# Openings of a fused two-block kernel: several output tiles side by side while h's rows come, x in four transfers and squared as it lands

## The reference, cut to what matters

```python
h = rmsnorm(x, norm_gain)                  # x * rsqrt(mean(x*x) + 1e-6) * gain
proj = h @ w_in                            # 1024 x 7956, split over four mixers
...                                        # four mixers -> ys
mixed = sum(sigmoid(merge[i]) * (ys[i] @ w_branch[i]))
x = rmsnorm(x + mixed @ w_out, final_gain)
for l in range(2):                         # second block, two layers
    h = rms_norm(x, norm_mix_g[l]) * (1 + scale_m) + shift_m
    proj = h @ w_in[l]                     # queries, keys, values, gates
    ...                                    # two attentions, gates, w_out
    x = x + gate_m * y
    h = rms_norm(x, norm_mlp_g[l]) * (1 + scale_f) + shift_f
    x = x + gate_f * (relu(h @ w_mlp_up[l])**2 @ w_mlp_down[l])
```

## Time and profile before

| | us |
|---|---|
| median of 3 runs | 2796.71 (2793.35 to 2798.49) |
| the profiled execution's own time | 2806.41 |
| its span, first to last instruction | 2804.7 |
| PE busy in the span | 2584.9 (92%) |
| DVE busy | 1627.1 (58%) |
| ACT busy | 1056.1 (38%) |
| mean granted TensorE clock | 0.952 of full speed |

### The profile page before, as it was taken

How to read it: one execution, slowest core, us unless ns; L and a number is a source line. 1 busy time by engine, 2 the same in 40 slices (tenths; PEclk the granted TensorE clock), 3 DMA queues, 4 the chain that set the end, 5 groups by cost and what they waited for, 6 DMA issues and landing times. The chain is left out here.

```text
span 2804.7 us, 37803 instructions
## 1 busy us (share of the span) xinstructions
PE 2584.9 (92%) x14861; PEld 2061.8 (74%) x14861; DVE 1627.1 (58%) x3102; ACT 1056.1 (38%) x2170; POOL 22.1 (1%) x68
## 2 busy tenths in 40 slices
PE   6998687899989999889989999898999899899999
PEld 4886577688767668767768888687577677688887
DVE  5645666887665686343477775563873533544444
ACT  3235422433455365442332222353653522422221
POOL 0001000000000000000000000000000000000000
PEclk8997898899989999999999999899999999899999
DMA  4220110576312201303335553121003032223220
GB/s 152 80 60 1 35 35 3 187 219 199 124 60 65 90 1 46 81 25 98 108 136 192 196 192 108 60 91 60 31 16 87 26 94 90 89 90 113 98 91 30
DMA packets 212218, 249.42 MB, mean 89 GB/s; under 512 B 13551, under 2 KB 125898, under 8 KB 212042
## 3 DMA queue, kind: packets, MB, share of 16 engines
q1 hardware_dynamic: 185504, 195.87, 21.8%
q10 hardware_dynamic: 26538, 51.14, 5.3%
HBM read 243.57 MB, written 2.10 MB: 88 GB/s over the span
## 5 line engine op out<-in xcount | busy, mean ns | idle before, releaser
L2558 ACT ACTIVATE weights_hi<-weight_ring 128x512 fp32r<-128x512 f32 (+1 forms) x240 | 143.8, 603 | 402.2 <-PE bank L2614 374.5
L2580 DVE TENSOR_TENSOR weights_lo<-weight_ring,weights_hi 128x512 fp32r<-128x512 f32 (+1 forms) x240 | 155.5, 652 | 223.4 <-ACT weights_hi L2558 223.3
L3205 ACT ACTIVATE weights_hi<-weight_ring 128x1024 fp32r<-128x1024 f32 x128 | 135.3, 1057 | 257.1 <-PE bank L3300 255.8
L2614 PE MATMUL bank<-h_hi,weights_hi 128*128 128x512 f32 x512 | 208.9, 408 | 14.8 <-DVE h_lo L2580 8.5
L3300 PE MATMUL bank<-h_hi,weights_hi 128*128 128x512 f32 x512 | 203.1, 397 | 13.2 <-DVE h_lo L422 12.3
L2614 PE MATMUL bank<-h_lo,weights_hi 128*128 128x512 f32 x512 | 204.4, 399 | 0.0
L3300 PE MATMUL bank<-h_lo,weights_hi 128*128 128x512 f32 x512 | 203.5, 397 | 0.0
L2775 PE MATMUL bank<-chunk_hi,h_hi 128*128 128x512 f32 x448 | 185.6, 414 | 18.1 <-DVE h_lo L422 15.5
L2614 PE MATMUL bank<-h_hi,weights_lo 128*128 128x512 f32 x512 | 202.0, 395 | 0.0
L3300 PE MATMUL bank<-h_hi,weights_lo 128*128 128x512 f32 x512 | 200.8, 392 | 0.0
L3300 PE MATMUL bank<-hidden_hi,weights_hi 128*128 128x512 f32 x512 | 199.4, 389 | 0.0
(11 more groups left out here) (495 smaller groups left out, 5407.5 us busy)
## 6 DMA issues: line engine op xcount, KB each, us to landing
arena<-in_ada_w ACTq DMA_DIRECT2D x48, 1024.0 KB, 5.2
weight_ring<-in_w_in SPq DMA_DIRECT2D x21, 2048.0 KB, 8.1
weight_ring<-in_w_in SPq DMA_DIRECT2D x65, 512.0 KB, 5.3
weight_ring<-in_w_mlp_up SPq DMA_DIRECT2D x16, 2048.0 KB, 9.2
weight_ring<-in_w_mlp_down SPq DMA_DIRECT2D x16, 2048.0 KB, 7.9
weight_ring<-in_w_out SPq DMA_DIRECT2D x6, 2048.0 KB, 7.9
weight_ring<-in_w_in SPq DMA_DIRECT2D x10, 1024.0 KB, 8.3
weight_ring<-in_w_branch_a SPq DMA_DIRECT2D x16, 512.0 KB, 6.4
```

Source lines behind the costliest of these rows:

```text
L2558: act.activation(hi, src, ACT.Copy).then_inc(*hi_done.one())
L2580: dve.tensor_tensor(lo, src, hi.bitcast(F32), ALU.subtract).then_inc(*lo_done.one())
L2614: ins = pe.matmul(out, ws[a_][:, n % PIECES, k - k0, :], tile["x"][b_][:, k, :], start=k + a_ + b_ == 0, stop=last[n] and k == k1 - 1 and ...
L3205: act.activation(ws[0][:, t % 2], src[t // 4][:, :, c % 4 * P:c % 4 * P + P], ACT.Copy)\
```

## The change

x comes in four transfers of 256 columns each, PE transposes as they land, and ACT squares and DVE adds each row behind its copy, in `load`. The block `rms` is gone: the product with ones, the mean and the root stand at the head of `first_projection`, and the first chunk's weights are split between h's rows. In `first_projection` PE works on the first chunk's four tiles side by side: for each row k, 12 matmuls. In `queries_keys` with a norm it works on three units side by side (9 matmuls per row), and turns lag 3 steps in place of 2. In `mlp` it works on two tiles side by side (6 per row); both weight splits are made first. In `split_products` with a norm DVE scales rows 0 to 3, makes piece 0's splits, and scales rows 4 to 7 after them.

```diff
 # load
-                pe.wait_ge(*self.x_landed.all_of_stage(16))
                 for k in range(ND):
+                    if k % (ND // PARTS) == 0:
+                        pe.wait_ge(*self.x_parts[k * PARTS // ND].at(16))
...
                     dve.tensor_copy(self.xT[:, k, :], self.bank[k][:]).then_inc(*self.evac_dve.one())
+                    if k >= 2:
+                        squares.add(dve, k - 1)
+                squares.add(dve, ND - 1)
...
+                act.preload_act_table_set(LN_AND_EXP)
+                for k in range(ND):
+                    act.wait_ge(*self.evac_dve.at(k + 1))
+                    squares.square(act, k, self.xT[:, k, :])
...
-                sp.dma_start(x_tm, a["x"][0].rearrange("(i p) d -> p i d", p=P)).then_inc(*self.x_landed.dma())
+                for j in range(PARTS):
+                    cols = slice(j * width, (j + 1) * width)
+                    sp.dma_start(x_tm[:, :, cols], a["x"][0].rearrange("(i p) d -> p i d", p=P)[:, :, cols])\
+                      .then_inc(*self.x_parts[j].dma())
-    def rms(self, name, gain, rs):
...
 # first_projection
+                norm.sums(pe)
+                opening = last.index(True) + 1
...
+                for k in range(ND):
+                    pe.wait_ge(*h_split.at(k + 1))
+                    self.w.wait_parts(pe, ("p1", name), k)
+                    for t in range(opening):
+                        lo = tiles[t][3]
+                        for a_, b_ in ((0, 0), (1, 0), (0, 1)):
+                            ins = pe.matmul(self.bank[t][:], w[b_][:, k, lo:lo + P], h[a_][:, k, :], start=k + a_ + b_ == 0,
+                                            stop=k == ND - 1 and b_ == 1)
...
+                self.w.split_hi(act)
+                norm.root(act)
                 for k in range(ND):
+                    if k % 2 == 0 and k < ND - 2:
+                        self.w.split_hi(act)
                     norm.first_part(act, h[0][:, k, :], k).then_inc(*h_first.one())
...
+                norm.mean(dve)
+                self.w.split_lo(dve)
+                norm.vector_and_second(dve, second, piece)     # piece: split_lo at k 2, 4, 6
...
 # split_products
-                if norm is not None:
-                    norm.vector(dve)
+                for k in range(ND // 2 if norm is not None else 0):
+                    norm.vector_row(dve, k)
...
+                    for k in range(ND // 2, ND if norm is not None and n == 0 else 0):
+                        norm.vector_row(dve, k)
...
 # queries_keys
+                def opening():
+                    for k in range(ND):
+                        pe.wait_ge(*h_split.at(k + 1))
+                        self.w.wait_parts(pe, key, k)
+                        for i in range(3):
...
-                steps((0, project), (2, turn), beside=lambda step: guest.tensor(pe, step))
+                if norm is None:
+                    steps((0, project), (2, turn), beside=lambda step: guest.tensor(pe, step))
+                else:
+                    opening()
+                    steps((0, lambda n, c, i: project(n, c, i) if n >= 3 else None), (3, turn))
...
 # mlp
                 split(0)
+                split(1)
                 self.norm.root(act)
...
-                    if t + 1 < N:
+                    if t and t + 1 < N:
                         split(t + 1)
...
+                split(0)
                 self.norm.mean(dve)
-                split(0)
+                split(1)
...
+                for k in range(ND):
+                    pe.wait_ge(*lo_done.at(k + 3))
+                    for t in range(2):
+                        for a_, b_ in ((0, 0), (0, 1), (1, 0)):
+                            ins = pe.matmul(self.bank[t][:], ws[a_][:, t, k, :], hs[b_][:, k, :], start=k + a_ + b_ == 0,
+                                            stop=k == ND - 1 and a_ == 1)
```

More of the change, by code:

```diff
@@ L345, in __init__ @@
         self.scaled, self.shifted = kernel.scaled, kernel.shifted
-        self.squares, self.first_mean = squares, first_mean
+        self.squares, self.first_mean, self.open = squares, first_mean, True
     def sums(self, pe):
@@ L380, in vector_row @@
     def vector_row(self, dve, k):
-        if k == 0 and self.squares is not None:
+        if k == 0 and self.open:
             dve.wait_ge(*self.kernel.root_done.at(1))
@@ L883, in __init__ @@
         self.x_landed = Signal(nc, "x_landed")
+        self.x_parts = [Signal(nc, f"x_part_landed_{j}") for j in range(4)]
         self.mm_done = Signal(nc, "mm_done")
@@ L968, in load @@
         rows = self.take(2, P)
+        PARTS = 4
+        width = D // PARTS
+        squares = Squares(self)
         with nc.Block() as block:
@@ L1022, in load @@
         self.end_stage("load")
-    def rms(self, name, gain, rs):
[L1028 to L1063, removed]
-                    self.w.split_lo(dve)
-                dve.wait_ge(*self.mm_done.at(1))
-                dve.tensor_scalar(rs, self.bank[0][:], 1.0 / D, EPS, ALU.mult, ALU.add)\
-                   .then_inc(*self.dve_ready.step("mean"))
-                for _ in range(pieces - pieces // 2):
-                    self.w.split_lo(dve)
-            @block.sync
-            def _(sp):
-                self.w.feed(sp)
-        self.top = keep
-        self.end_stage(name)
@@ L1078, in first_projection @@
+        return squares
     def first_projection(self):
@@ L1167, in _ @@
             def _(pe):
+                norm.sums(pe)
+                name = tiles[0][0]
+                opening = last.index(True) + 1
+                w = self.w.parts(("p1", name))
+                assert opening <= NB and all(tile[1] == "features" for tile in tiles[:opening])
+                for k in range(ND):
[6 more added lines that the diff above has]
+                                            stop=k == ND - 1 and b_ == 1)
+                        if k == ND - 1:
+                            ins.then_inc(*self.mm_done.one())
+                self.w.release(self.mm_done)
                 for t, (name, kind, i, lo, n) in enumerate(tiles):
+                    if t < opening:
+                        continue
                     key = ("p1", name)
@@ L2748, in queries_keys, with steps @@
         h, h_first, h_split = self.split_h, self.shifted, self.pool_ready
-        def steps(*stages, beside):
+        def steps(*stages, beside=None):
             for step in range(max(N + max(lag for lag, _ in stages), guest.LAST if guest else 0)):
@@ L2779, in project @@
                         self.w.release(pe_done)
+                def opening():
+                    key = chunks[0][0]
+                    w = self.w.parts(key)
+                    for k in range(ND):
+                        pe.wait_ge(*h_split.at(k + 1))
+                        self.w.wait_parts(pe, key, k)
+                        for i in range(3):
+                            for a_, b_ in ((0, 0), (1, 0), (0, 1)):
+                                ins = pe.matmul(self.bank[i][:, 0:width], h[a_][:, k, i * P:(i + 1) * P], w[b_][:, k, :],
+                                                start=k + a_ + b_ == 0, stop=k == ND - 1 and b_ == 1)
+                            if k == ND - 1:
+                                ins.then_inc(*pe_done.one())
                 def turn(n, c, i):
```

32 lines of the change are left out of this document (17 added, 15 removed).

## The result

| | before | after |
|---|---|---|
| median, us | 2799.43 (10 runs, 2793.35 to 2808.32) | 2791.51 (10 runs, 2789.29 to 2800.36) |
| ratio after / before | | 0.9968, 95% interval 0.9957 to 0.9979 |
| span of the profiled execution | 2804.7 | 2789.9 |
| mean granted clock | 0.952 | 0.957 |

The change is faster by 0.32% by the ratio, 9.0 us with an interval from 5.9 to 12.0, and by 7.9 us between the two medians; I had forecast 11.9 us and 2784.8. The two profiled spans differ by 14.8 us, nearly twice what the medians say, so a single pair of traces can't be read as the result. I go through the stages first and come back to this.

A forecast was written before the change was run, and what follows sets the result against it. PE, 92% busy, was taken to bound the kernel. Terms -8.9 - 4.5 - 5.1 + 2.65 + 2.1 + 1.85 = -11.9 us, off 2796.7, gave 2784.8 us; range 2777 to 2792.5.

The forecast's parts named there:

- The start: Load to h's first row: quartered x brings that row at 21.7 against 29.25, 7.5 us earlier; bounds 6 and 9.
- The fixed cost of about 2.0 us: x's transfers: if paid in series, the last quarter lands about 6 us later and the sum is about -9.5.
- The first projection's opening: First projection, four tiles side by side: done at 48.2 against 57.1, -8.9 us, 7.5 of them from the earlier start.
- The low clock: Start of an opening: 3.7 us at low clock from its first matmul, 8.7 matmuls, when PE always has work.
- Queries and keys: Queries and keys, both layers, three units side by side: -4.5 and -5.1 us net, from 6.7 and 7.2 saved.
- what is given back: Behind the queries' openings: waits of 0.4 for a scale, 1.3 for a weight piece, 0.45 for the later turn; 2.15 together.
- Rival C: All openings: the clock stays at 0.5 through them, +58 us less 11.9, giving 2843; chance 0.03.
- Merge: Merge: four rows scaled behind the guest's transfer make each later piece 2.65 us later, +2.65 us.
- Feed-forwards: Feed-forwards, both layers: two tiles side by side and the queue ahead of tile 2 cost +2.1 and +1.85 us.
- A: Behind openings: queue longer than counted, queries and keys giving back 4 to 5 us each, feed-forwards 3; 2792; chance 0.19.
- B: Merge and weight queue cost nothing and the start gives its upper bound: -17.5, 2779; chance 0.12.
- D: Start: x's quarters land together with weights, the last at 26 in the worst case; +2, 2799; chance 0.04.

The follow-up runs named there:

- e3: Kernel after with both merge's eight rows scaled at once and the feed-forwards of before; 2781.80 us, ratio to before 0.9934.
- e7: Kernel after with x in one transfer in place of four; 2795.46 us, ratio to before 0.9981.
- e6: Kernel after with the first projection's tiles one after another, tile 0 alone row by row, new start kept; 2796.27 us, ratio to before 0.9979.
- e1: Kernel after with merge scaling all eight rows first, as before; 2788.21 us, ratio to before 0.9958.
- e9: Kernel after, unchanged, run again for a second trace; 2791.18 us, ratio to before 0.9963.
- e2: Kernel after with the feed-forward stage of before; 2781.88 us, ratio to before 0.9938.
- e4: Kernel before with only the new opening of queries and keys; 2792.17 us, ratio to before 0.9968.
- e8: Kernel before, unchanged, run again for a second trace; 2801.96 us, ratio to before 1.0000.
- e10: Kernel after with merge's rows and feed-forwards as before, plus three unused extra products per sum of squares in all five openings; 2779.06 us, ratio to before 0.9929.
- e12: Kernel before with three unused extra products after the sums of squares in queries and keys and feed-forwards; 2800.34 us, ratio to before 0.9998.

## Why the prediction was right, and by how much each step was off

**How right.** 2791.5 lies inside the range of 2777 to 2792.5, 1.0 us from its upper end, and outside the 2781 to 2789 to which I gave 0.62. That the steps add up to 11.6 us, so near to the 11.9 said, is in part luck: the first projection and the queries gained 2.5 us more than I said, the merge and the feed-forwards cost 2.8 more.

**The start: right, 1.3 us early.** I said 21.7 for h's first row; it was 20.42. Copy and addition take 1.20 a pair, not 1.36: back to back, an instruction of 0.68 starts 0.60 after the one before it. And the first quarter landed at 4.50, not 5.3. The last one landed later than I took (10.33, not 9.2), and that was as harmless as I said: in e3 it landed at 9.02, and h's first row came at 20.52, no earlier. Against x whole (9.08 in e7) the last quarter was 1.25 us later in this trace, and from 0.06 earlier to 1.6 later in four others. The fixed cost of about 2.0 us in the Trainium skill's "DMA: Bandwidth & Descriptors", section "Anatomy of one DMA", is stated there for a transfer on the path of gpsimd, and x's transfers are issued by SP. That several of them pay it one behind another was my own reading; by that estimate the last quarter would have been 6 us later, and the traces don't agree with it.

**The first projection's opening: right in size (-8.9 said, -9.3 in the first trace, -10.0 between the means), wrong in its account.** I gave the start 7.5 of it and the order 1.4. By e6 the order is worth 6.5, by e7 the quarters 4.2; the parts aren't additive, since the new place of the weight splits makes a one-tile opening slower than before's. The low clock lasted 5.3 us and not 3.7, which the earlier start made up; over the traces with this opening it was 3.7 to 6.0.

**Queries and keys: right, gain too small.** -4.5 and -5.1 said; -5.5 and -5.5 between the means. The openings themselves gained 6.6 us each in the first trace, near the 6.7 and 7.2 that I counted; mis-sized was what is given back, 0.3 and 0.6 in place of 2.15. I had counted a wait of 0.4 for a scale, which isn't there, and 1.3 for a weight piece, which is 0.67 and 0.71. Rival C is refuted: the clock was at 1.0 from 3.7 us (layer 0) and 4.8 us (layer 1) on. For these openings the order that the Trainium skill's "TensorE: Matmul & The Clock Gate", section "Why this matters for your kernels", asks for with thin outputs, K-contiguous, is not the one that raised the clock: all tiles of one k, without a gap, raised it, while one tile's k after k, with gaps, stayed at 0.50 for 14.8 us (e6). The section speaks of waits for transfers between K-tiles; here PE waits for DVE's rows.

**Merge: right.** +2.65 said, +2.8 found, by the mechanism said (e1). The idle time was 3.69 in the first trace and not 3.2, since the transfer came 6.4 us after the first row's start and not 5.9; in five others it was 2.5 to 2.7.

**Feed-forwards: the mis-sized term.** +2.1 and +1.85 said, 3.95 together; 6.6 between the means of the steps. The wait ahead of tile 2 was what I said ("about 3 us"; 3.04 and 3.03). The opening's length was not: I took 12.8 us; in layer 0 PE went from 1415.87 to 1429.61 (1432.65 less the wait), 13.7, the clock being low for 5.2 us and not 3.7, which by 0.46 us each makes 0.7 of the 0.9. And I had not thought of one case: at the wait the clock can fall (e9, e6); e9's +6.0 alone makes 0.6 us of layer 1's mean. In time, undoing this part gave 9.6 us (e2 against after) and 6.4 (e3 against e1); by the intervals of the ratios each difference is uncertain by some 6 us, so the times show that this part costs, and not how much.

**Time against sum.** 2791.5 against 2784.8 is 6.7 us: 2.7 because the ten runs of before have a median of 2799.43, and the three that I had 2796.71; and 4.0 because the medians differ by 7.9, not 11.9. The steps of the traces give 11.6, so the 4 us are not missing from the openings as traced. Nor are they clear of noise: by the ratio the change is worth 9.0 us, with an interval of 5.9 to 12.0 that holds 11.9, and e9's group gives 9.1 between the medians and 10.4 by its ratio. Whether the rest is chance, or a clock that falls at the feed-forwards' waits more often in timed executions than in two of ten traced ones, stays open. e4 speaks against the second: it has the feed-forwards of before, and its steps exceed its time by 4 to 5 us as well.

**Rivals.** A (2792) came closest in the number, but only half by its mechanism: the feed-forwards did cost its 3 us each, while the queue behind the queries' opening was shorter than I counted, where A wanted it longer. B is refuted, though the start came near its upper bound (8.8 us of its 9): merge and the weight queue cost what I said or more. D is refuted: the last quarter came at 10.33, not at 26.

## What to carry to other kernels

Where rows come slower than one tile uses them and faster than all tiles do, give PE several tiles per row; it pays where PE is the limit afterwards (queries, projection), and costs where two tiles end together in front of two buffers and a serial emptying queue (feed-forward). Before splitting a block of work into a part before and a part behind a wait, look at whether it stands in that wait already. And judge a change of 0.3% by steps of single stages in several traces: the first pair of spans differed by 14.8 us and the second (2803.7 and 2799.6, e8 and e9) by 4.1, for a change that is worth 8 to 9 in time.

## What the runs showed of the hardware

- The preparations, which no kernel here changes, took 5 to 6 us less in six of thirteen traces, at the same matmuls: in the part that before ran from 210 to 262 us the clock was low for 24 to 27 us in place of 34.
- At waits of 3.03 to 3.05 us in front of a dense stretch the granted clock stayed at 1.0 in eight of ten cases. In two it fell to 0.5: once 1 us behind the wait, for 3.4 us (e6), and once 0.9 us before its end, for 6.8 us (e9).
- With PE busy on extra products until 0.63 us ahead of an opening, the opening ran at 1.00 from its first matmul (e10). Where PE then waited for rows, in e12's queries, the clock fell again 6.9 and 8.4 us into the opening.
- Openings in which PE always had work stayed at 0.5 for times that differ from trace to trace: 3.0 to 6.0 us in the queries.
